# Two moves of waiting work in a one-core transformer kernel: the masks and suffix sums of the stick-breaking mixer, and the bias lines of the first feed-forward

## The reference, cut to what matters

```
y = x * rsqrt(mean(x * x) + 1e-6) * g          # _rmsnorm
ffn = (silu(y @ w_gate) * (y @ w_up)) @ w_down # 2816 hidden columns
```

## Time and profile before

| | us |
|---|---|
| median of three runs | 4114.15 |
| the profiled execution, whole | 4120.59 |
| its span | 4118.9 |
| TensorE matmul busy | 3952.5 (96%) |
| VectorE busy | 2740.5 (67%) |
| ScalarE busy | 1988.3 (48%) |
| GpSimd busy | 174.9 (4%) |

### The profile page before, as it was taken

How to read it: one execution, slowest core, us unless ns; L and a number is a source line. 1 busy time by engine, 2 the same in 40 slices (tenths; PEclk the granted TensorE clock), 3 DMA queues, 4 the chain that set the end, 5 groups by cost and what they waited for, 6 DMA issues and landing times.

```text
span 4118.9 us, 78738 instructions
## 1 busy us (share of the span) xinstructions
PE 3952.5 (96%) x34162; PEld 3832.3 (93%) x34162; DVE 2740.5 (67%) x4076; ACT 1988.3 (48%) x2624; POOL 174.9 (4%) x216
## 2 busy tenths in 40 slices
PE   8989999899998999989998999999999999999999
PEld 7978999899997899978987899999999899999999
DVE  6566665666655656556644699965855689984865
ACT  4445454454443545455433544754444554664443
POOL 0011000110000000001001200000000000000000
PEclk9999999899999999999988999999999999999999
DMA  5534555345455455533542255455754355445754
GB/s 218 193 112 144 195 186 194 119 145 194 170 193 173 144 195 185 194 113 133 195 149 103 103 185 195 172 186 209 253 195 175 127 182 194 174 176 204 260 200 163
DMA packets 119641, 720.80 MB, mean 175 GB/s; under 512 B 14064, under 2 KB 19840, under 8 KB 37632
## 3 DMA queue, kind: packets, MB, share of 16 engines
q1 hardware_dynamic: 91296, 660.64, 45.5%
q10 hardware_dynamic: 26400, 43.28, 3.0%
q0 software_dynamic: 1600, 11.83, 0.7%
HBM read 692.48 MB, written 23.22 MB: 174 GB/s over the span
## 4 chain that ended last, share of the span: by engine, by line
PE 85%; DVE 7%; ACT 4%; issue 2%; DMA 1%; ACTq 1%; DVEq 0%
PE psum L658 26%; PE psum L659 25%; PE psum L660 25%; PE psum L1386 3%; DVE slab_low L1911 2%; ACT slab_high L1407 2%; PE psum L1050 1%; DVE h_parts L2199 1%; PE psum L1033 1%; PE psum L1063 1%; ACT room L1661 0%; PE psum L874 0%; DVE room L1934 0%; ACTq L1570 0%; PE psum L1327 0%
## 5 line engine op out<-in xcount | busy, mean ns | idle before, releaser
L1911 DVE TENSOR_TENSOR slab_low<-slab,slab_high 128x2048 fp32r<-128x2048 f32 x622 | 1424.7, 2291 | 839.4 <-ACT slab_high L1407 836.9
L658 PE MATMUL psum<-h_parts,slab_high 128*128 128x256 f32 x5632 | 1584.9, 281 | 54.1 <-DVE h_parts L2199 39.3
L1407 ACT ACTIVATE slab_high<-slab 128x2048 fp32r<-128x2048 f32 x630 | 1191.0, 1891 | 872.9 <-PE psum L660 758.6
L659 PE MATMUL psum<-h_parts,slab_high 128*128 128x256 f32 x5632 | 1563.7, 278 | 0.0
L660 PE MATMUL psum<-h_parts,slab_low 128*128 128x256 f32 x5632 | 1563.1, 278 | 0.0
L658 PEld LDWEIGHTS psum<-h_parts,slab_high 128*128 128x128 f32 x5632 | 1070.7, 190 | 75.8 <-issue 45.9
L658 PE MATMUL psum<-hidden_parts,slab_high 128*128 128x256 f32 x3840 | 1067.0, 278 | 19.0 <-DVE hidden_parts L2146 4.8
L659 PEld LDWEIGHTS psum<-h_parts,slab_high 128*128 128x128 f32 x5632 | 1070.7, 190 | 2.6 <-issue 2.4
L660 PEld LDWEIGHTS psum<-h_parts,slab_low 128*128 128x128 f32 x5632 | 1070.3, 190 | 0.0
L659 PE MATMUL psum<-hidden_parts,slab_high 128*128 128x256 f32 x3840 | 1061.5, 276 | 0.0
L660 PE MATMUL psum<-hidden_parts,slab_low 128*128 128x256 f32 x3840 | 1061.4, 276 | 0.0
(11 more groups left out here) (326 smaller groups left out, 3332.0 us busy)
## 6 DMA issues: line engine op xcount, KB each, us to landing
slab<-in_up SPq DMA_DIRECT2D x176, 1024.0 KB, 4.8
slab<-in_keys_up SPq DMA_DIRECT2D x128, 1024.0 KB, 4.8
slab<-in_keys_down SPq DMA_DIRECT2D x128, 1024.0 KB, 4.8
slab<-in_down SPq DMA_DIRECT2D x88, 1024.0 KB, 4.8
slab<-in_w_in SPq DMA_DIRECT2D x16, 1024.0 KB, 4.8
slab<-in_wq SPq DMA_DIRECT2D x16, 1024.0 KB, 4.9
peer_gates<-room ACTq DMA_DIRECT2D x64, 256.0 KB, 2.3
room<-peer_gates ACTq DMA_DIRECT2D x64, 256.0 KB, 5.4
```

The source lines that it names most:

```text
L658: nc.tensor.matmul(out, lhs[0], rhs[0], start=first, stop=False, **options)
L659: nc.tensor.matmul(out, lhs[0], rhs[1], start=False, stop=False, **options)
L1407: nc.scalar.activation(k.high[m % PARTS][:, 0:width], k.slabs[m % RING][:, 0:width], ACT.Copy).then_inc(k.rounded.up())
L1911: nc.vector.tensor_tensor(k.low[m % RING][:, 0:width], k.slabs[m % RING][:, 0:width], k.high[m % PARTS][:, 0:width], ALU.subtract).then_in ...
```

## The change

Two independent edits. First, in the mixer, VectorE masks both pairs of a group before it makes the low part of the next slab (it did so behind it), and TensorE does the suffix sums after 12 of a tick's 24 matmuls (it did them ahead of all 24). Second, in the first feed-forward, TensorE does the bias lines behind f = 5 and VectorE copies them in tick 6. The wait for the copies goes from f = 3 to f = 7, the next pair that uses the same banks, and the fill of the masked row stays in tick 1. With the low part of the slab, two other operations of VectorE's tick that stood between it and the masks (the root chain in tick 2, the scaling of a projection out of PSUM) also come behind the masks.

```diff
@@ TensorE.ffn
             if f < 4 and at == k.sum_pair:
                 nc.tensor.wait_ge(k.meaned.sem, k.meaned.at(1))
-                if first:
-                    nc.tensor.wait_ge(k.lines_copied.sem, 1)
+            if first and f == 7:
+                nc.tensor.wait_ge(k.lines_copied.sem, 1)
...
-            if f == 1 and first:
-                nc.tensor.wait_ge(k.meaned.sem, k.meaned.at(1))
+            if f == 5 and first:
+                nc.tensor.wait_ge(k.up_scaled.sem, k.up_scaled.at(4))
                 self.bias_lines()
@@ TensorE: the loop over stick_heads(tick, 4), unchanged, becomes suffixes(v, tick)
+    def suffixes(self, v, tick):
...
-                self.project_half(n, half, k.banks[n % 3], v.jobs[n][1])
+                self.project_half(n, half, k.banks[n % 3], v.jobs[n][1], lambda: self.suffixes(v, tick))
...
-                self.mixed_half(v, n - len(v.jobs), half)
+                self.mixed_half(v, n - len(v.jobs), half, lambda: self.suffixes(v, tick))
@@ TensorE.project_half and mixed_half (between=lambda: None)
         for c in range(DC):
+            if c == DC // 2:
+                between()
@@ VectorE.ffn and bias_lines
             if tick == 1 and first:
+                nc.vector.memset(k.bias_views.table[32:33, :], MASKED).then_inc(k.table_filled.up())
+            if tick == 6 and first:
                 self.bias_lines()
...
-        nc.vector.memset(b.table[32:33, :], MASKED).then_inc(k.table_filled.up())
         nc.vector.wait_ge(k.lines_made.sem, 1)
@@ VectorE.stick, in each tick
-            if half == 0 and n < len(v.jobs) + DC // 2:
-                self.rest_slab()
...
             for pair in [2 * g + e for g, at in enumerate(STICK_AT) if tick == at + 2 for e in range(2)]:
...
                 nc.vector.tensor_tensor(z[:, :, T:STICK_W], z[:, :, T:STICK_W], strict, ALU.mult).then_inc(k.masked.up())
+            if half == 0 and n < len(v.jobs) + DC // 2:
+                self.rest_slab()
...
```

More of the change, by code:

```diff
@@ L895, in conv_sum @@
             mm.then_inc(k.conv_summed.up())
+    def suffixes(self, v, tick):
+        k, nc = self.k, self.k.nc
+        for hd in stick_heads(tick, 4):
+            bank = k.banks[(7, 4)[hd % 2]]
+            nc.tensor.wait_ge(k.masked.sem, k.masked.at(hd // 2 + 1))
+            if hd % 4 >= 2:
+                nc.tensor.wait_ge(k.summed_up.sem, k.summed_up.at(hd - 1))
+            nc.tensor.matmul(bank[:, 0:T], k.const("later"), v.z[:, hd % NP, 0:T], start=True, stop=False, skip_group_check=True)
+            nc.tensor.matmul(bank[:, P:T], k.const("ones"), v.z[:, hd % NP, T:STICK_W], start=False, stop=True, skip_group_check=True)
+            nc.tensor.matmul(bank[:, T:STICK_W], k.const("later"), v.z[:, hd % NP, T:STICK_W], start=True, stop=True,
+                             skip_group_check=True).then_inc(k.suffixed.up())
     def stick(self, v):
@@ L915, in stick @@
                 mm.then_inc(k.valued.up())
[L916 to L924, removed]
             for hd in stick_heads(tick, 0):
@@ L948, in stick, with project_half @@
                     nc.tensor.wait_ge(k.columns_scaled.sem, k.columns_scaled.at(4))
-                self.mixed_half(v, n - len(v.jobs), half)
+                self.mixed_half(v, n - len(v.jobs), half, lambda: self.suffixes(v, tick))
             if tick == 1:
                 self.sums(v)
-    def project_half(self, n, half, bank, by_token=0):
+    def project_half(self, n, half, bank, by_token=0, between=lambda: None):
         k, nc = self.k, self.k.nc
@@ L979, in project_half, with mixed_half @@
             mm.then_inc(k.slab_done.up())
-    def mixed_half(self, v, j, e):
+    def mixed_half(self, v, j, e, between=lambda: None):
         k, nc = self.k, self.k.nc
@@ L2179, in stick @@
                 nc.vector.tensor_tensor(z[:, :, T:STICK_W], z[:, :, T:STICK_W], strict, ALU.mult).then_inc(k.masked.up())
+            if half == 0 and n < len(v.jobs) + DC // 2:
+                self.rest_slab()
+            if tick == 2:
+                self.early_root(v)
+            if half == 0 and 1 <= n <= len(v.jobs) and (n - 1) % 3 == 1:
+                bank = k.banks[(n - 1) % 3].rearrange("p (a t) -> p a t", a=2)
+                nc.vector.wait_ge(k.slab_done.sem, k.slab_done.at(n))
+                nc.vector.tensor_tensor(v.jobs[n - 1][0], bank, v.rstd[:, 0:T].unsqueeze(1).to_broadcast([P, 2, T]), ALU.mult).then_inc(k.columns_scaled.up())
             for pair in stick_pairs(tick, 7):
```

## The result

The changed kernel took 4083.47 us (median of four runs, 4081.62 to 4090.95), the kernel before 4114.12 us. The ratio is 0.9921 with a 95% interval of 0.9909 to 0.9934: 30.7 us faster, where I had predicted 9 us and a range that ended at 4100.5. A second measurement on another occasion gave the same ratio (0.9921, 0.9907 to 0.9934).

What follows compares the result with a forecast made beforehand. TensorE, busy for 96% of the span, was taken to bound the kernel. A first feed-forward gain of 9.6 us and a mixer cost of 0.4 summed to -9.2 us, from 4114.15 to 4105, with a range from 4100.5 to 4110.

Steps and rivals of the forecast that it cites:

- The failed step: Mixer: tick 10 needs the low part made behind the masks, so TensorE starts at 1785.60 instead of 1785.50; +0.4 us in four groups.
- the agreement of two sums: Mixer, first group: old order (masks last) and new order (low part last) end within 0.1 us of each other.
- the mixer's clock: Mixer: time at the lower clock covers 4 to 5 us of work in either order, so no gain.
- the forecast's mechanism: Mixer: VectorE makes masks first, then the low part TensorE waits for; four waits of 5 to 6.5 us stay.
- The new wait for slab 3: First feed-forward: TensorE waits 0.41 us before f = 3 in place of the old 6.18 us, net gain 5.77 us.
- The skewed copy: First feed-forward: the large DRAM copy, issued some 17 us later, makes slab 10 land 1 to 3 us later, inside 4.6.
- rival 3: First feed-forward: the skewed copy stops the loads, 4.9 us lost and some 2 us of clock; 4112, no change; 6%.
- The sum of 10.14 us: First feed-forward, profiled execution: 5.77 from the wait, 1.34 from the bias lines' clock, 3.03 from f = 2 at full clock.
- The typical value of 9.6: First feed-forward: gain expected in the median, 0.5 us below the profiled sum because the lower clock typically lasts some 4.8 us.
- Rival 1: Mixer: the stall does shrink, TensorE starting 2.2 us earlier in each of four groups, 8.8 us, 4096; 7%.
- Rival 4: Mixer: value products wait for GpSimd behind the later sums, 2.4 us plus 2 us of clock per group; 4122 to 4123; 5%.
- Its cover: Mixer: slack before the values need GpSimd's mask, 3.6 us against 2.0 (first pair), 2.2 against 1.4 (last group).

## Why the prediction was wrong

**The failed step** is in the mixer: "And TensorE needs just this low part for tick 10, because the products now stand ahead of the sums in the tick." The low part of tick 8 is that of job 6, which tick 12 takes. The description of the kernel ahead of the prediction has the same mistake ("In tick 2n VectorE makes the low part of the slab of job n + 1"; it is job n + 2). I had counted the one call of `rest_slab` ahead of all stages and not the second one, inside `early_input` of the first feed-forward (`if first and c == FIRST_LAG`). From there on every stage prepares two slabs ahead. In the first stage I had used the right lead ("Slab 4: VectorE can start at about 34.4" is the low part of its tick 2), and in the mixer the wrong one, without setting the two side by side.

The trace of before could have told. A slab is rounded at the earliest when the one three before it is used up. ScalarE's rounding in tick 6 before, in its timeline:

```profile
1765.99 1.91 ACT L1407 ACTIVATE slab_high<-slab 128x2048 fp32r<-128x2048 f32 x1 [3.85 <-PE psum L660]
```

It waited for TensorE, which ended tick 5, and with it job 2, just before the scores of 1765.8. What job 2 releases is the slab of job 5. So tick 6 prepares job 5, tick 8 job 6, and the low part of 1780.49 is not the one that tick 10 needs. I never read this releaser. Instead I used the agreement of two sums (1785.5 both ways) as if it confirmed the pairing. It was a coincidence. The wrong step also put the mixer's clock at nothing in the sum.

With the lead of two, the forecast's own numbers give the result. The first pair's masks start with the first logarithm and take 2.66 us. TensorE arrives later by the 12 matmuls. After: masks out at 1775.41, TensorE there at 1775.1, a wait of 0.35. In the three other groups there is none, since their logarithms come earlier against TensorE's tick. That removes 21.9 - 0.4 = 21.5 us of wait. The rest of the sum, from the lists of waits of the stage: 28.2 us in all before (21.9, 2.1, 1.6, 1.5, 1.1), 10.3 after, so 17.9 of the 23.7 us are waits. The other 5.8 are TensorE's busy time (131.87 to 126.07 us), the same matmuls at a higher clock. Granted clock over the mixer, before:

```profile
1742.95:1903.05 160.10, 131.87 (x999) 123.41 (x998) 92.11 (x125) 84.56 (x99) 19.67 (x19) 0.91 0.30 106
```

0.91 against 0.96 after. The run with the preparation one job later closes the argument: there the forecast's mechanism appears with its predicted size, 6.75 us where the forecast has 6.6 (TensorE's wait of 6.53 before and 0.1 more), and the mixer is back at 160.3 us.

**The first feed-forward was right** in its mechanism and within 0.7 us in size. Timeline of TensorE after, which answers to the earlier trace rows:

```profile
33.41 0.39 PE L658 MATMUL psum<-h_parts,slab_high 128*128 128x256 f32 x1 [0.20 <-DVE slab_low L1919]
...
49.98 0.81 PE L764 MATMUL psum<-consts,room 33*8 33x384 f32 x2
50.62 0.80 PE L765 MATMUL psum<-consts,room 33*8 33x384 f32 x2
51.36 0.39 PE L658 MATMUL psum<-h_parts,slab_high 128*128 128x256 f32 x1
```

The new wait for slab 3 ends at 33.41 (predicted 33.38). The lines take 51.36 - 49.98 = 1.38 us (predicted 1.3, before 2.64), and no TensorE instruction waited for them. The clock held, at 1.00 from 28 to 50 us. What the forecast had too short is the stream itself: f = 3 to f = 5 took 49.98 - 33.41 = 16.57 us instead of 16.32, and f = 6 some 0.3 us more than 5.44. VectorE scaled f = 6 at 57.16, where 56.5 was predicted and 66.63 measured before:

```profile
54.76 0.54 DVE L2027 COPY room<-psum 8x384 f32<-8x384 f32 x1
...
57.16 0.69 DVE L2005 TENSOR_TENSOR room<-psum,room 128x512 f32<-128x512 f32 x1 [1.19 <-PE psum L660]
```

The copies ended at 55.30 (predicted 54.9), ahead of f = 7. The skewed copy met more loads, as feared, and landed after 13.0 us instead of 11.1. Slab 10 came through on time. It was slab 11, released when f = 7 was done at 62.6, that was rounded only at 72.0, and that is 9.4 us where slab 6 had 7.5. The view of DMA issues, and ScalarE's timeline:

```profile
room<-bias_lines POOLq DMA_DIRECT2D x1, 2048.0 KB, 13.0
```

```profile
72.00 1.93 ACT L1415 ACTIVATE slab_high<-slab 128x2048 fp32r<-128x2048 f32 x1 [6.81 <-DMA slab<-in_up]
```

TensorE waited for no load (rival 3 did not come). The sum of 10.14 us came out as 9.47 in the profiled pair. The typical value of 9.6 stands against 9.5 by the run of this edit alone, whose interval is wide (5.8 to 13.6 us). The stage with its old code took 205.15 to 206.85 us in five executions (that of before, and four with edits elsewhere), and 197.13 to 197.49 in seven with the new: 8.3 us between the medians, less than the 9.6, so that the lower clock in the profiled execution of before was on its long side, as I had allowed for.

**The rivals.** Rival 1 (the stall in the mixer shrinks, 4096, 7%) was the one that came, for the reason that it names ("It needs a low part that comes earlier than I think"), and with more than twice the 8.8 us that I gave it (23.7): I had let TensorE wait for both pairs' masks and had given the clock nothing. Rival 4 priced the chain behind the later sums. Its cover was thinner than I wrote: the value products waited 1.3 us in three groups for GpSimd, because the low part of tick 8 now stands in front of the additions on VectorE and the sums come 12 matmuls later. With the sums ahead of all matmuls the same low part held up the second sums (the 3.2 us above) and GpSimd nothing. Timeline of GpSimd after, which answers to the earlier trace rows:

```profile
1782.15 1.84 POOL L2658 TENSOR_TENSOR room<-room,consts 128x256 f32<-128x256 f32 x1 [36.59 <-ACT room L1625]
1783.95 0.73 POOL L2659 TENSOR_TENSOR room<-room,consts 128x256 f32<-128x256 f32 x1
```

The first mask took 1.84 us with VectorE's L1919 running from 1781.11, as before the change. VectorE's low part beside it took its usual 2.28 us, so what I derived from the Trainium skill ("SBUF — State Buffer", "Who interferes with whom") for the low part, a delay of up to 1.1 us, did not show: VectorE had started first.

## What to carry to other kernels

Before a forecast rests on which buffer an instruction fills, count the fills and the uses from a point where the pairing is certain, and let one row confirm the count; two times that agree do not confirm a pairing. In an engine that works in order, put work that has slack of a whole job behind work that somebody waits for: the place of one such line was worth 25 us of the mixer's 160, and three more places took another 4 to 8 us off it. A wait of 5 to 6 us on TensorE cost more than itself here, because matmuls behind it ran at half speed for some microseconds: 15.8 us of waits less made 9.6 us of matmul time less as well.

## What the runs showed of the hardware that was not expected

The same code with the same waits differs by 4.2 us in one stage (132.23 against 136.44 us) through TensorE's clock alone, 1.00 against 0.96. In the execution at 0.96 the matmuls went to the lower level at 1839.40, 1.5 us behind the end of a wait of 1.91 us in tick 24. The run of the mixer's two edits alone had the same wait and the same fall, 1.5 us behind its end. The execution at 1.00 had the same wait of 1.91 us and no fall. That the wait brought the fall is likely and not shown. If it did, waits that short cost more than themselves in some executions and not in others. Either way, kernels that differ by less than 5 us in a stage must be compared by their lists of waits as well as by its length.
